# Conformer convolution and its layer norm: a tenth tap moved off VectorE, the mean's channel sums and the squares' sums moved to TensorE

## The chip, the cores and the metric

The kernel runs on one core of one Trainium2 chip. The metric is the device time of one execution in microseconds (us). A core has TensorE (PE, with its weight loads shown apart as PEld), VectorE (DVE), ScalarE (ACT), GpSimd (POOL) and the DMA queues, most of them fed by SyncE (SP). An engine works through its own instructions in order, and semaphores tie the engines together.

## What is computed

A model of two conformer and attention layers, followed by a mixer layer, on 512 latent tokens and 256 context tokens with 1024 channels. The part that matters is the first layer's convolution module:

```
u = h @ w_pw1 + b_pw1
a, g = split(u, 2)
v = a * sigmoid(g)
v = dwconv(v, w_dw, b_dw)            # 31 taps along the tokens, one weight for each tap and channel
v = silu(layernorm(v, ln_g, ln_b))   # mean and variance over the 1024 channels of a token
y = v @ w_pw2 + b_pw2
```

Latent and context tokens go through it as two separate sequences of 512 and 256.

## The kernel before

**Layout.** Activations lie with the channels on the 128 partitions: a tile of the 8 channel tiles is 128 channels by 768 tokens (512 latent, 256 context). Sums over channels are therefore sums over partitions, which TensorE makes by a matmul with a matrix of ones (`ones`), and sums over the 8 tiles.

**Stage `pw1`.** `pw1_pe` multiplies the 16 weight chunks of `w_pw1` (two for each channel tile: gate, then value) in three fp32r products each (high and low parts, lines 593 to 595). Between the chunks it works off the modulation weights (`ada`, line 818), two or three groups of 64 matmul records in each period. `sigmoid` on ScalarE and `gated` on VectorE (line 1267) make the gated tile `vp[j]`. Then the 31 taps of tile j are divided as follows: one on TensorE with a diagonal matrix (`taps_pe`, line 880), which opens the sum in PSUM; 9 (`POOL_TAPS`) as a product on ScalarE (`tap_act`, line 1311, two instructions for each tap) with the sum on GpSimd (`sum_pool`, line 1322, 8 sums for each tile); and 21 (`DVE_TAPS`) on VectorE (line 1290, two instructions for each tap, of 512 and of 256 tokens). VectorE puts `gated(j + 1)` after its 12th tap and ends the tile by adding GpSimd's sum (line 1294). `copy_conv` on ScalarE (line 1371) then writes `cv[j]` and frees the PSUM pair for the value chunk of tile j + 2. Products wait in a ring of three buffers (`PT_RING`), so a tap product waits for the sum three before it. ScalarE's order in a tile is five taps, the sigmoid, a weight chunk's high part, `copy_conv(j - 1)`, the modulation rows with their DMAs, the other taps, and the second weight chunk before the last of them. GpSimd also makes the low parts of the weights (line 535), the diagonal for TensorE (line 1394), and, one tile late, the running sum of `cv` over the channel tiles (`cv_sum_pool`).

**Between `pw1` and `pw2`.** After a last pair of transposes that wait for modulation values read back by DMA (line 842), `mean_pe` multiplies `ones` with `cv_sum` (tiles 0 to 6) and, once `cv[7]` is there, with `cv[7]` (line 1385). `mean_dve` subtracts the mean from the 8 tiles (line 1434), `square_act` squares them (line 1008), `add_square_dve` adds the squares tile by tile (line 1017), and `norm_pe` sums them over the channels with `ones` (line 988), so that all 128 partitions hold the same 768 sums. ScalarE takes the root of all 128 x 768 (line 1158), VectorE the reciprocal of all of it (line 1186), and VectorE multiplies tile by tile (line 1197). ScalarE applies gain, shift and SiLU (line 1176) and writes the high part (line 1178), VectorE the low part (line 1193), and `pw2`'s matmuls start with the first tile.

**The rest.** After `pw2` comes a long row of matmul stages; their weights are streamed chunk by chunk: SP loads `raw`, ScalarE makes the high part, GpSimd the low part, TensorE multiplies.

Of the kernel before, what the change touches and what calls it, by code (L numbers as in the profile page):

```python
# [6 lines left out]
P = 128  # L7
D = 1024
# [8 lines left out]
TAPS = 31  # L17
PAD = TAPS // 2
PE_TAPS = 1
POOL_TAPS = 9  # L20
PT_RING = 3
EPS = 1e-6
GN_EPS = 64e-5
# [129 lines left out]
class Program:  # L153

    def __init__(self, nc, ctx, A):
# [9 lines left out]
        def at(name, offset, shape, dt=F32):  # L166
            return nc.alloc_sbuf_tensor_at(name, [P] + shape, dt, offset=offset)
# [18 lines left out]
        self.cv_sum = at("cv_sum", r_wlo, [2, HALF * P])[:, :, KD * P:HALF * P]  # L186
# [193 lines left out]
def build_in(nc, ctx, A, out, stop):  # L380
# [770 lines left out]

    def norm_act(act, name):
        i, pair, w = NN[name], norm_pair(name), NORM_W[name]
        if name not in EARLY.values():
            for k in range(KD):
                square_act(act, name, k)
        act.wait_ge(stat_ready, done(i + 1))
        act.activation(M.n_y[:, 0, 0:w], M.pair(pair, 0, w), ACT.Sqrt, scale=1.0 / D, bias=eps_col)\
            .then_inc(rms_ready, 1)
        if name == "n10":  # L1160
            for g in (0, 1):
                group_act(act, g, 0, g * 1024)
            high_first(act)
            act.wait_ge(mod_ready, done(1))
        for k in range(KD):
            act.wait_ge(t_ready, done(8 * i + k + 1))

            if k >= 2:
                act.wait_ge(x_ready, done(8 * i + k - 1))
            else:  # L1170
                act.wait_ge(rstd_ready, done(i + 1))
            fn = ACT.Silu if name == "ln" else ACT.Identity
            dst = M.n_y[:, k % 2, :]
            for s, t0, t1 in norm_segs(name):
                scale, shift = scale_of(name, k, s)
                ins = act.activation(dst[:, t0:t1], M.n_t[:, k % 2, t0:t1], fn, scale=scale, bias=shift)
            act.drain()
            act.activation(M.x_hi[:, k, 0:w], M.n_y[:, k % 2, 0:w], ACT.Copy).then_inc(y_ready, 1)

    def norm_dve(dve, name):  # L1180
        i, pair, w = NN[name], norm_pair(name), NORM_W[name]
        if name not in EARLY.values():
            for k in range(KD):
                add_square_dve(dve, name, k)
        dve.wait_ge(rms_ready, done(i + 1))
        dve.reciprocal(M.pair(pair, 0, w), M.n_y[:, 0, 0:w]).then_inc(rstd_ready, 1)  # L1186
        dve.wait_ge(rstd_ready, done(i + 1))
# [12 lines left out]
        low(KD - 1)  # L1200
# [196 lines left out]
    def cv_sum_pool(pool, j):  # L1397
        def halves(k):
            return M.cv[:, k, :].rearrange("p (a b) -> p a b", a=2)

        if j < 1:
            return
        pool.wait_ge(cv_ready, done(j + 1))
        if j == 1:
            pool.tensor_tensor(M.cv_sum, halves(0), halves(1), ALU.add).then_inc(cv_sum, 1)
            return
        pool.wait_ge(cv_sum, done(j - 1))
        pool.tensor_tensor(M.cv_sum, M.cv_sum, halves(j), ALU.add).then_inc(cv_sum, 1)

    def pw1_pool(pool):  # L1410
        pool.wait_ge(start_c, done(3 + KD))
# [2 lines left out]
        for j in range(8):  # L1414
            for n in range(1, 5):
                sum_pool(pool, j, n)
            if j < 6:
                low_stream(pool, "pw1", 2 * j + 4, 2 * j + 5)
            sum_pool(pool, j, 5)
            sum_pool(pool, j, 6)  # L1420
            cv_sum_pool(pool, j - 1)
            if j < 7:
                diag_pool(pool, j + 1)
            for n in range(7, POOL_TAPS):
                sum_pool(pool, j, n)
            if j < 6:
                low_stream(pool, "pw1", 2 * j + 5, 2 * j + 6)
# [1593 lines left out]

    @block.tensor
    def _(pe):
        prime(pe, [pe_taps, mod_t, tile_done, ada_used, start_t, stat_ready, mu_ready, mem_t, out_t, mix_stat, ffn2_stat, rope_r, turn_t, att_s, att_t, att_o, T_S.sem])
        start_pe(pe)
        for st in order:
            if st == "ln":
                mean_pe(pe)
            if st == "n10":
                ada_pe(pe)  # L3030
            elif st in NN:
                norm_pe(pe, st)
            if st == "w_in":
                w_in_pe(pe)
# [101 lines left out]
```

## Time and profile before

| | |
|---|---|
| median of 3 runs | 2482.0 us (2481.49 to 2483.29) |
| profiled execution, its own time | 2475.95 us |
| its span (first to last instruction) | 2474.2 us |
| TensorE busy | 2249.4 us, 91% of the span |
| VectorE, ScalarE, GpSimd busy | 1201.3, 985.8, 814.3 us |
| mean granted TensorE clock | 0.954 of full speed |

The rows of the trace give times from the start of the span. A timeline row is: start, length, engine, line, operation, output <- inputs, shapes, count of merged instructions, and in brackets the idle time of the engine ahead of it with what ended it.
### The profile page before, as it was taken

The numbers are of one execution on the slowest core, as the hardware profiler recorded it, in microseconds if no ns is written. First come the engines' busy times: TensorE is split into PE (matmuls) and PEld (weight loads), VectorE is DVE, ScalarE is ACT, GpSimd is POOL, SyncE is SP. The second block draws the span as 40 slices with busy tenths as digits, with TensorE's granted clock in tenths as the row PEclk, the third lists the DMA queues.
The fourth block names the chain that finished last, engine by engine and source line by source line (L and its number), as shares of the span: only waits on it lengthen the run. The fifth ranks groups of instructions, "written<-read, shape, count | busy, mean of one in ns | idle before, by whom it ended". The sixth has DMA issues, their size and how long they took to land.

```text
span 2474.2 us, 36592 instructions
## 1 busy us (share of the span) xinstructions
PE 2249.4 (91%) x14159; PEld 1844.7 (75%) x14159; DVE 1201.3 (49%) x2038; ACT 985.8 (40%) x1634; POOL 814.3 (33%) x391
## 2 busy tenths in 40 slices
PE   5999297999999996989979999989988879999998
PEld 4887186888888885867758888877756767778777
DVE  4799834432034325468554313458565435541441
ACT  5555445332133314368544324444453213441441
POOL 1788221323223221300124434433302113444443
PEclk9999598999999998999989999999988879999999
DMA  8887011222122221200023333332200002233332
GB/s 267 268 261 240 19 52 43 60 68 71 58 60 60 73 63 48 77 18 1 27 85 94 104 87 99 108 103 77 81 1 2 2 1 77 85 106 88 87 101 86
DMA packets 337086, 204.54 MB, mean 83 GB/s; under 512 B 5869, under 2 KB 335159, under 8 KB 336951
## 3 DMA queue, kind: packets, MB, share of 16 engines
q1 hardware_dynamic: 331915, 194.02, 26.2%
q10 hardware_dynamic: 5036, 8.66, 1.1%
q8 instruction: 91, 1.49, 0.3%
q14 instruction: 44, 0.36, 0.0%
HBM read 200.47 MB, written 2.19 MB: 82 GB/s over the span
## 4 chain that ended last, share of the span: by engine, by line
PE 49%; issue 27%; DVE 11%; POOL 8%; ACT 2%; DVEq 1%; SPq 1%; DMA 1%; ACTq 0%; POOLq 0%
PE ps L593 14%; PE ps L594 14%; PE ps L595 14%; POOL w_lo L535 7%; DVE ps L1290 6%; PE ps L1622 1%; DVE ps L1186 1%; DVE m L2820 1%; PE ps L1650 1%; PE ps L2639 1%; DMA ada_x<-in_ada_w 1%; SPq L696 0%; PE ps L2635 0%; PE ps L2626 0%; PE ps L818 0%
## 5 line engine op out<-in xcount | busy, mean ns | idle before, releaser
L535 POOL TENSOR_TENSOR w_lo<-raw,w_hi 128x1024 fp32r<-128x1024 f32 (+1 forms) x253 | 646.5, 2556 | 1394.4 <-ACT w_hi L565 1378.4
L593 PE MATMUL ps<-x_hi,w_hi 128*128 128x512 f32 (+1 forms) x1864 | 679.4, 364 | 63.3 <-DVE x_lo L1193 50.6
L594 PE MATMUL ps<-x_lo,w_hi 128*128 128x512 f32 (+1 forms) x1864 | 666.8, 358 | 0.0
L595 PE MATMUL ps<-x_hi,w_lo 128*128 128x512 f32 (+1 forms) x1864 | 665.8, 357 | 0.0
L565 ACT ACTIVATE w_hi<-raw 128x1024 fp32r<-128x1024 f32 (+1 forms) x251 | 280.6, 1118 | 559.4 <-PE ps L595 553.9
L593 PEld LDWEIGHTS ps<-x_hi,w_hi 128*128 128x128 f32 x1864 | 355.7, 191 | 134.2 <-issue 60.6
L594 PEld LDWEIGHTS ps<-x_lo,w_hi 128*128 128x128 f32 x1864 | 356.0, 191 | 52.9 <-issue 3.8
L595 PEld LDWEIGHTS ps<-x_hi,w_lo 128*128 128x128 f32 x1864 | 355.4, 191 | 51.2
L1523 DVE SCALAR_TENSOR_TENSOR f_a<-ps,prm,f_a 128x511 f32<-128x511 f32 (+2 forms) x176 | 116.2, 681 | 356.3 <-ACT f_b L1488 345.4
L593 PE MATMUL ps<-g_hi,w_hi 128*128 128x512 f32 (+1 forms) x704 | 256.9, 365 | 2.1 <-POOL w_lo L535 1.4
L594 PE MATMUL ps<-g_lo,w_hi 128*128 128x512 f32 (+1 forms) x704 | 255.8, 363 | 0.0
L595 PE MATMUL ps<-g_hi,w_lo 128*128 128x512 f32 (+1 forms) x704 | 255.4, 363 | 0.0
L1290 DVE SCALAR_TENSOR_TENSOR ps<-vp,prm,ps 128x512 f32<-128x512 f32 x336 | 177.8, 616 | 2.5 <-PE ps L880 2.5
L1488 ACT ACTIVATE f_a<-ps,prm 128x512 f32<-128x512 f32 (+1 forms) x66 | 56.2, 851 | 300.2 <-PE ps L595 212.2
L593 PEld LDWEIGHTS ps<-g_hi,w_hi 128*128 128x128 f32 x704 | 132.8, 189 | 25.4 <-POOL w_lo L535 3.0
L595 PEld LDWEIGHTS ps<-g_hi,w_lo 128*128 128x128 f32 x704 | 132.7, 188 | 21.2
L593 PE MATMUL ps<-xg_hi,w_hi 128*128 128x512 f32 x352 | 139.7, 397 | 9.3 <-POOL w_lo L535 9.3
L594 PEld LDWEIGHTS ps<-g_lo,w_hi 128*128 128x128 f32 x704 | 132.9, 189 | 20.1
L595 PE MATMUL ps<-xg_hi,w_lo 128*128 128x512 f32 x352 | 137.2, 390 | 0.0
L594 PE MATMUL ps<-xg_lo,w_hi 128*128 128x512 f32 x352 | 137.2, 390 | 0.0
L1322 POOL TENSOR_TENSOR pc<-pc,pt 128x768 f32<-128x768 f32 x64 | 118.0, 1843 | 27.2 <-ACT pt L1311 21.9
L1555 DVE SCALAR_TENSOR_TENSOR h<-ps,mods,h 128x512 f32<-128x512 f32 (+1 forms) x48 | 30.3, 659 | 188.3 <-PE ps L595 188.3
(363 smaller groups left out, 2907.5 us busy)
## 6 DMA issues: line engine op xcount, KB each, us to landing
raw<-in_ffn_w_up SPq DMA_DIRECT2D x88, 512.0 KB, 3.8
ada_tail<-in_ada_w SPq DMA_DIRECT2D x22, 1024.0 KB, 7.4
raw<-in_ffn_w_down SPq DMA_DIRECT2D x32, 704.0 KB, 4.4
raw<-in_w_up SPq DMA_DIRECT2D x44, 512.0 KB, 3.8
ada_s<-in_ada_w SPq DMA_DIRECT2D x20, 1024.0 KB, 7.8
raw<-in_conv_w_pw SPq DMA_DIRECT2D x24, 512.0 KB, 6.4
raw<-in_w_down SPq DMA_DIRECT2D x16, 704.0 KB, 4.4
raw<-in_w_in SPq DMA_DIRECT2D x17, 512.0 KB, 3.9
```

The lines of the kernel that those rows point to most:

```text
L535: pool.tensor_tensor(M.w_lo[:, slot, 0:K * P], M.raw[:, slot, 0:K * P], M.w_hi[:, slot, 0:K * P].bitcast(F32), ALU.subtract).then_inc(lo_r ...
L565: act.activation(M.w_hi[:, slot, 0:K * P], M.raw[:, slot, 0:K * P], ACT.Copy).then_inc(hi_ready, 1)
L593: pe.matmul(o, wh, hi[:, k, t0:t0 + tn], start=(k == 0), stop=False)
L594: pe.matmul(o, wh, lo[:, k, t0:t0 + tn], start=False, stop=False)
L595: return pe.matmul(o, wl, hi[:, k, t0:t0 + tn], start=False, stop=(k == K - 1))
L1186: dve.reciprocal(M.pair(pair, 0, w), M.n_y[:, 0, 0:w]).then_inc(rstd_ready, 1)
L1290: dve.scalar_tensor_tensor(out=o, in0=src, scalar=w, in1=o, op0=ALU.mult, op1=ALU.add)\
L1322: pool.tensor_tensor(acc, acc, M.pt[:, m % PT_RING, :], ALU.add).then_inc(pool_tap, 1)
L1488: ins = act.activation(dst[:, slot, 0:w], M.pair(pr, 0, w), ACT.Identity, scale=ffn_cols(b, zero_tap, t, hf, j), bias=ffn_cols(b, None, t, ...
L1523: ins = dve.scalar_tensor_tensor(out=dst[:, slot, o0:o1], in0=M.pair(pr, o0 + sh, o1 + sh), scalar=ffn_cols(b, tap, t, hf, j), in1=dst[:, ...
L1555: dve.scalar_tensor_tensor(out=o, in0=src, scalar=M.mods[:, 48 * b + 40 + m, s:s + 1], in1=o, op0=ALU.mult, op1=ALU.add)
L1622: mm = pe.matmul(M.pair(u % 2, off, off + n), lhs, rhs, start=first, stop=True, skip_group_check=True)
```

## The change

Three edits, all in the convolution module.

1. `POOL_TAPS` is 10 instead of 9, so VectorE has 20 taps for each tile, ScalarE 10 products and GpSimd 9 sums. ScalarE's second weight chunk stays ahead of the last product.
2. The running sum `cv_sum` on GpSimd goes away (7 sums, their semaphore and their buffer). `mean_pe` multiplies `ones` with each of `cv[0]` to `cv[7]`.
3. In the layer norm the squares are no longer added by VectorE. TensorE multiplies each tile of squares, as the moving operand in six blocks of 128 tokens, with a stationary matrix of 128 x 6 that has ones in one column and zeros elsewhere (`pick6`), and so puts the sums of block b into row b of a PSUM tile of 6 x 128. Root and reciprocal work on 6 x 128. Six matmuls with a row of the identity, stretched to 6 x 128, put each row back on all 128 partitions.

```
-POOL_TAPS = 9
+POOL_TAPS = 10
...
-        pe.wait_ge(cv_sum, done(6))
-        for t0, t1, half in ((0, 384, 0), (384, SEQ, 1), (SEQ, TOK, 1)):
-            pe.matmul(M.pair(pair, t0, t1), ones, M.cv_sum[:, half, ...], start=t0 != 384, ...)
-        pe.wait_ge(cv_ready, done(KD))
-        for t0, tn in BOTH:
-            mm = pe.matmul(M.pair(pair, t0, t0 + tn), ones, M.cv[:, KD - 1, t0:t0 + tn], ...)
+        for k in range(KD):
+            pe.wait_ge(cv_ready, done(k + 1))
+            for t0, tn in BOTH:
+                mm = pe.matmul(M.pair(pair, t0, t0 + tn), ones, M.cv[:, k, t0:t0 + tn], start=(k == 0),
+                               stop=(k == KD - 1))
         mm.then_inc(mu_ready, 1)
+
+    def ln_pe(pe):
+        i = NN["ln"]
+        pe.wait_ge(evac, done(NORM_Q["ln"]))
+        for k in range(KD):
+            pe.wait_ge(sq_ready, done(8 * i + k + 1))
+            for b in range(6):
+                mm = pe.matmul(ln_rows(), M.pick6[:, 5 - b:11 - b], M.n_sq[:, k % 2, b * P:(b + 1) * P],
+                               start=(k == 0 and b == 0), stop=(k == KD - 1 and b == 5))
+            mm.then_inc(sq_used if k < KD - 1 else stat_ready, 1)
+        pe.wait_ge(ln_rt, done(1))
+        for b in range(6):
+            mm = pe.matmul(M.pair(norm_pair("ln"), b * P, (b + 1) * P), ident[0:6, b:b + 1].to_broadcast([6, P]),
+                           ln_row(0), start=True, stop=True)
+        mm.then_inc(ln_back, 1)
+
+    def ln_square_act(act, k):
+        ...
+        act.wait_ge(cv_cent, done(k + 1))
+        if k >= 2:
+            act.wait_ge(sq_used, done(7 * i + k - 1))
+        act.activation(M.n_sq[:, k % 2, :], M.cv[:, k, :], ACT.Square).then_inc(sq_ready, 1)
+
+    def ln_root_act(act):
+        act.wait_ge(stat_ready, done(NN["ln"] + 1))
+        act.activation(ln_row(1), ln_rows(), ACT.Sqrt, scale=1.0 / D, bias=M.one[0:6, 0:1]).then_inc(ln_sd, 1)
+
+    def ln_root_dve(dve):
+        dve.wait_ge(ln_sd, done(1))
+        dve.reciprocal(ln_row(0), ln_row(1)).then_inc(ln_rt, 1)
+        dve.wait_ge(ln_back, done(1))
...
             if k >= 2:
                 act.wait_ge(x_ready, done(8 * i + k - 1))
-            else:
-                act.wait_ge(rstd_ready, done(i + 1))
+            elif name != "ln":
+                act.wait_ge(rstd_ready, done(i + (i < 2)))
...
-            sum_pool(pool, j, 5)
-            sum_pool(pool, j, 6)
-            cv_sum_pool(pool, j - 1)
+            for n in range(5, 8):
+                sum_pool(pool, j, n)
             if j < 7:
                 diag_pool(pool, j + 1)
-            for n in range(7, POOL_TAPS):
+            for n in range(8, POOL_TAPS):
                 sum_pool(pool, j, n)
...
+        pool.memset(M.pick6[:, :], 0.0)
+        pool.drain()
+        pool.memset(M.pick6[:, 5:6], 1.0)
         pool.drain().then_inc(zero_ready, 1)
```

The last four lines stand at the very start of GpSimd's program; SP and ScalarE wait for `zero_ready`. For `ln`, `ln_square_act` and `ln_root_act` take the place of the squares and the root in `norm_act`, and `ln_root_dve` that of the additions and the reciprocal in `norm_dve`.

## Rows read from the trace of the kernel before

**Rows 1.** Chain of work that ended last, from 106.5 to 306 us, by line

```profile
by line: DVE ps L1290 74.5%; issue 6.3%; DVE cv L1434 3.5%; DVE n_t L1017 3.4%; DVE vp L1267 3.1%; DVE ps L1186 2.5%; PE ps L1385 1.5%; PE ps L988 1.5%; ACT L1176 0.6%; DVE ps L1294 0.6%; ACTq L1177 0.5%; DVE x_lo L1193 0.5%; ACT cv L1371 0
```

**Rows 2.** Timeline of VectorE in `pw1`: starts of tiles 1, 2 and 7

```profile
106.51 12.70 DVE L1290 SCALAR_TENSOR_TENSOR ps<-vp,prm,ps 128x512 f32<-128x512 f32 x24 [0.23 <-PE ps L880]
...
130.61 12.70 DVE L1290 SCALAR_TENSOR_TENSOR ps<-vp,prm,ps 128x512 f32<-128x512 f32 x24
...
251.11 22.14 DVE L1290 SCALAR_TENSOR_TENSOR ps<-vp,prm,ps 128x512 f32<-128x512 f32 x42
```

**Rows 3.** Timeline of TensorE in `pw1`: taps of tiles 1, 3 and 7, and a wait

```profile
104.94 1.46 PE L880 MATMUL ps<-vp,diag 128*128 128x512 f32 x4
...
151.05 1.46 PE L880 MATMUL ps<-vp,diag 128*128 128x512 f32 x4
...
155.97 0.47 PE L593 MATMUL ps<-x_hi,w_hi 128*128 128x512 f32 x1 [1.58 <-ACTq L1373]
...
240.80 2.48 PE L880 MATMUL ps<-vp,diag 128*128 128x512 f32 x4 [2.06 <-DVE vp L1267]
```

**Rows 4.** Groups by line and form, 70 to 275 us: busy, mean ns, idle before

```profile
L1322 POOL TENSOR_TENSOR pc<-pc,pt 128x768 f32<-128x768 f32 x64 | 118.0, 1843 | 27.2 <-ACT pt L1311 21.9
L535 POOL TENSOR_TENSOR w_lo<-raw,w_hi 128x1024 fp32r<-128x1024 f32 x16 | 38.3, 2398 | 25.7 <-ACT w_hi L565 25.7
...
L1311 ACT ACTIVATE pt<-vp,prm 128x512 f32<-128x512 f32 x64 | 45.7, 714 | 16.8 <-issue 9.4 <-POOL pc L1322 7.4
```

**Rows 5.** Timeline of all engines, 256 to 306 us

```profile
256.84 3.77 POOL L1322 TENSOR_TENSOR pc<-pc,pt 128x768 f32<-128x768 f32 x2 [6.16 <-ACT pt L1311]
259.02 0.33 ACTq L871 DMA_DIRECT2D mod_t<-mod_scratch  x1
...
261.32 0.50 PE L842 MATMUL ps<-kb,mod_t 80*128 80x80 f32 x2 [15.46 <-DMA mod_t<-mod_scratch]
...
275.23 2.93 PE L1385 MATMUL ps<-cv,kb 128*128 128x512 f32 x4 [9.81 <-ACT cv L1371]
...
278.19 7.01 DVE L1434 SCALAR_TENSOR_TENSOR cv<-ps,cv 128x768 f32<-128x768 f32 x8 [2.79 <-PE ps L1385]
279.24 0.84 ACT L1008 ACTIVATE n_t<-cv 128x768 f32<-128x768 f32 x1 [4.06 <-DVE cv L1434]
...
291.27 1.28 ACT L1158 ACT_TABLE_LOAD   x1
...
292.59 2.90 PE L988 MATMUL ps<-n_t,kb 128*128 128x512 f32 x4 [14.43 <-DVE n_t L1017]
...
296.46 4.96 DVE L1186 RECIPROCAL ps<-n_y 128x768 f32<-128x768 f32 x1 [4.02 <-ACT n_y L1158]
...
301.50 1.28 ACT L1176 ACT_TABLE_LOAD   x1 [5.07 <-DVE ps L1186]
...
305.87 0.76 PE L593 MATMUL ps<-x_hi,w_hi 128*128 128x512 f32 x1 [10.38 <-DVE x_lo L1193]
```

**Rows 6.** Busy time in stretches: PE, PEld, DVE, ACT, POOL, granted clock, DMA, GB/s

```profile
305.87:309.40 3.53, 3.53 (x10) 2.95 (x11) 3.35 (x4) 3.40 (x4) 0.00 (x0) 0.50 0.00 0
309.40:320.00 10.60, 10.08 (x59) 8.69 (x58) 8.43 (x10) 8.26 (x10) 0.00 (x0) 0.99 0.00 0
...
2025.00:2030.00 5.00, 5.00 (x25) 4.57 (x24) 0.00 (x0) 0.00 (x0) 0.00 (x0) 0.50 0.00 0
```

**Rows 7.** Timeline of TensorE elsewhere: fp32 records over 128 columns, weights of 6 columns

```profile
1084.74 0.60 PE L1637 MATMUL ps<-kb,p 128*128 128x128 f32 x4
...
1734.02 0.09 PEld L2152 LDWEIGHTS ps<-hot,relb 33*6 33x6 f32 x2 [0.35 <-issue]
```

**Rows 8.** Groups by line and form, whole span: a smaller reciprocal and a smaller copy

```profile
L1127 DVE RECIPROCAL rm<-rm 128x256 f32<-128x256 f32 x1 | 1.8, 1754 | 2.9 <-ACT rm L1118 2.9
L856 ACT ACTIVATE mod_rows<-ps 128x256 f32<-128x256 f32 x12 | 4.6, 383 | 6.7 <-PE ps L818 3.2 <-issue 2.6 <-ACT cv L1371 0.9
```

**Rows 9.** Chain of work that ended last, the first microseconds of the kernel

```profile
1.64 0.23 POOLq L2959
```

More of the change, by code:

```diff
@@ L426, in build_in @@
     pe_taps = sem("pe_taps")
-    cv_sum = sem("cv_sum")
+    ln_sd = sem("ln_sd")
+    ln_rt = sem("ln_rt")
+    ln_back = sem("ln_back")
     mu_ready = sem("mu_ready")
@@ L1153, in norm_act @@
         i, pair, w = NN[name], norm_pair(name), NORM_W[name]
-        if name not in EARLY.values():
+        if name == "ln":
             for k in range(KD):
[L1156 to L1159, printed above, removed]
+                ln_square_act(act, k)
+            ln_root_act(act)
+        else:
+            if name not in EARLY.values():
+                for k in range(KD):
+                    square_act(act, name, k)
+            act.wait_ge(stat_ready, done(i + 1))
+            act.activation(M.n_y[:, 0, 0:w], M.pair(pair, 0, w), ACT.Sqrt, scale=1.0 / D, bias=eps_col)\
+                .then_inc(rms_ready, 1)
         if name == "n10":
@@ L1181, in norm_dve @@
         i, pair, w = NN[name], norm_pair(name), NORM_W[name]
[L1182 to L1187, printed above, removed]
+        if name == "ln":
+            ln_root_dve(dve)
+        else:
+            if name not in EARLY.values():
+                for k in range(KD):
+                    add_square_dve(dve, name, k)
+            dve.wait_ge(rms_ready, done(i + (i < 2)))
+            dve.reciprocal(M.pair(pair, 0, w), M.n_y[:, 0, 0:w]).then_inc(rstd_ready, 1)
+            dve.wait_ge(rstd_ready, done(i + (i < 2)))
         if name == "n10":
@@ L1378, in mean_pe @@
         pe.wait_ge(evac, done(Q0["pw2"] - 4))
-        pe.wait_ge(cv_sum, done(6))
-        for t0, t1, half in ((0, 384, 0), (384, SEQ, 1), (SEQ, TOK, 1)):
-            pe.matmul(M.pair(pair, t0, t1), ones, M.cv_sum[:, half, t0 - 384 * half:t1 - 384 * half], start=t0 != 384,
-                      stop=False, skip_group_check=True)
-        pe.wait_ge(cv_ready, done(KD))
-        for t0, tn in BOTH:
-            mm = pe.matmul(M.pair(pair, t0, t0 + tn), ones, M.cv[:, KD - 1, t0:t0 + tn], start=False, stop=True,
-                           skip_group_check=True)
@@ L1387, in mean_pe, with ln_rows, ln_row @@
-        mm.then_inc(mu_ready, 1)
+        for k in range(KD):
+            pe.wait_ge(cv_ready, done(k + 1))
+            for t0, tn in BOTH:
+                mm = pe.matmul(M.pair(pair, t0, t0 + tn), ones, M.cv[:, k, t0:t0 + tn], start=(k == 0),
+                               stop=(k == KD - 1))
+        mm.then_inc(mu_ready, 1)
+    def ln_rows():
+        return M.pair((Q0["pw2"] + 1) % 4, 0, P)[0:6, :]
+    def ln_row(which):
+        return M.gate[0:6, 1, which * P:(which + 1) * P]
+    def ln_pe(pe):
+        i = NN["ln"]
+        pe.wait_ge(evac, done(NORM_Q["ln"]))
+        for k in range(KD):
+            pe.wait_ge(sq_ready, done(8 * i + k + 1))
[8 more added lines that the diff above has]
+        mm.then_inc(ln_back, 1)
@@ new lines, in ln_square_act @@
+    def ln_square_act(act, k):
+        i = NN["ln"]
+        if k == 0:
+            act.wait_ge(x_ready, done(8 * i))
+        act.wait_ge(cv_cent, done(k + 1))
[5 more added lines that the diff above has]
+        act.activation(ln_row(1), ln_rows(), ACT.Sqrt, scale=1.0 / D, bias=M.one[0:6, 0:1]).then_inc(ln_sd, 1)
@@ L1395, in diag_pool @@
         ins.then_inc(diag_ready, 1)
[L1397 to L1408, printed above, removed]
     def pw1_pool(pool):
@@ L2951, in _ @@
     def _(pool):
-        prime(pool, [P_S.sem, lo_ready, zero_ready, diag_ready, cv_sum, pool_tap, tap_prod])
+        prime(pool, [P_S.sem, lo_ready, zero_ready, diag_ready, pool_tap, tap_prod])
         pool.memset(M.p_rows[:, PT - 1, :], 0.0)
@@ L3028, in _ @@
                 mean_pe(pe)
+                ln_pe(pe)
             if st == "n10":
                 ada_pe(pe)
-            elif st in NN:
+            elif st in NN and st != "ln":
                 norm_pe(pe, st)
@@ L3069, in _ @@
     def _(dve):
-        prime(dve, [sq_used, evac, mod_ready, rstd_ready, t_ready, x_ready, h_ready, v_ready, tap_done, cv_cent,
+        prime(dve, [ln_rt, sq_used, evac, mod_ready, rstd_ready, t_ready, x_ready, h_ready, v_ready, tap_done, cv_cent,
                     taps_ready, prod_ready, g_ready, out_c, MIX.x, MIX.sum, MEMO.x, MEMO.sum, FFN2.x, FFN2.sum,
```

6 lines of the change are left out of this document (3 added, 3 removed).

## The prediction

> **What bounds the kernel now.** I read the page first (TensorE busy for 91% of the span), then the chain of waits over the part that the change touches, then the timelines. The chain [rows 1] shows that this part, unlike the rest, is not TensorE's: 74.5% of the 200 us from 106.5 to 306 us are VectorE's taps, and most of what is left is the layer norm, in which one engine at a time works. The timeline of VectorE [rows 2] shows the taps back to back: tile 1 starts at 106.51, tile 2 at 130.61, so a tile takes 24.10 us, and a tap (two instructions) takes 22.14 / 21 = 1.05 us. Tile 1 had to wait 0.23 us for TensorE's tap: up to there TensorE sets the pace. The timeline of TensorE [rows 3] shows it close behind afterwards: from its taps of tile 1 (104.94) to those of tile 3 (151.05) there are 46.11 us for two tiles, without a wait of note, 23.05 for each. From then on it waits for `copy_conv`, 1.58 us at 155.97. After the last tap there is a serial path [rows 5]: the mean ends at 278.16 (275.23 + 2.93), the squares' sums at 295.49, the reciprocal at 301.42, and `pw2` starts at 305.87. From there on TensorE is busy again (10.08 of 10.60 us, [rows 6]), so whatever `pw2`'s start gains, the end of the kernel gains: its weights are ready long before, and nothing in the later stages changes.
>
> **The tap.** It comes off each of 8 tiles on VectorE. For tile 0 it gives nothing: VectorE ends it earlier and then waits for TensorE's tap at 104.94 plus 1.46 [rows 3], so tile 1 still starts at 106.5. For tiles 1 to 7 it gives 1.05 each, 7.35 in all, if the others keep a period of 24.10 - 1.05 = 23.05. TensorE needs 23.05, exactly as much. Its waits for `copy_conv` go away when VectorE is earlier, since that is what they wait for, so it can hold this pace; I take off 0.15 for tiles at which the two meet: 7.2. ScalarE has one more tap, 0.71 for the 512 half plus an estimated 0.5 for the other [rows 4], of a tile in which it is busy for little more than half the time. GpSimd gets a sum of 1.84 and loses the running sum, an addition over the same 128 x 768, so it stays even: 9 x 1.84 + 2 x 2.40 [rows 4] plus a small diagonal, some 22 us of 23.05. The second weight chunk's high part slips by one product; it waits for a TensorE chunk anyway. Bounds of this term: 0 (rival C) and 8.05, the 7.35 plus the 0.23 and what tile 0 might still give.
>
> **The mean.** `cv_sum` was hidden, so taking it from GpSimd gains nothing by itself. What was exposed is one product over 768 tokens at 1.2 GHz, 2.93 us [rows 5]. Now there are eight. `cv[0]` to `cv[6]` can start when the transposes at line 842 are through, and those wait for a DMA that ScalarE issues behind its last products. That DMA went out at 259.02, when GpSimd's sums that started at 256.84 had begun to free the ring, and TensorE had its data 2.30 us later [rows 5]. In the changed kernel tile 7's sums start 6 x 1.05 = 6.3 earlier, at 250.5, and the tenth product waits for two of them (3.7), so the DMA goes out at about 254.3, the transposes run at 256.6 and the products start at 257.2. At 1.2 GHz a product costs 2.56 (2.93 without the last pass's tail, which I put at 0.35); at 2.4 GHz 1.39 (from 1.46 for the same four records, [rows 3]). The clock rises after some work: `pw2`'s first matmuls ran 3.53 us at 0.50 and then at 0.99 [rows 6]. With 3.5 us slow (1.4 products) and 5.6 products fast (7.8), TensorE is through `cv[6]` at 268.5. `cv[7]` is there at 275.2 - 7.2 = 268.0, so its product follows at once and ends at 270.1. Before, the mean came 2.96 us after `cv[7]` was there, now 2.1: gain 0.85. If the products stayed at 1.2 GHz throughout they would end at 257.2 + 8 x 2.56 + 0.35 = 278.0, and all that the taps gave would be gone. Bounds: +1.5 (7 products done in time, the last one fast) and -7.1.
>
> **The squares' sums.** From the first subtraction (278.19) to the end of the sum over channels (295.49) took 17.30. Seven additions on VectorE, about 1.06 apart, go. Now the first square is made as before, 1.05 behind the subtraction, and takes 0.84 [rows 5]; then 8 tiles of 6 matmuls, 96 records of 128 columns. Four such records with other weights took 0.60 [rows 7], so 0.11 apart behind a tail of 0.27; loading 6 columns takes 0.09 for two and hides. I take 0.115: 1.38 for a tile, 11.0 for all, plus 0.2. ScalarE's 0.84 for a square is hidden behind it, since two buffers alternate and TensorE is the slower. TensorE pauses for 1.9 us before it begins. After a pause of 2.06 us its four tap records took 2.48, not 1.46 [rows 3], so such a pause can drop the clock for a while; that costs 1.0 to 1.8, and I put in 0.9. Together 1.9 + 11.2 + 0.9 = 14.0: gain 3.3. Bounds: gain 4.2 (no dip), and at 1.2 GHz throughout 20.5 + 0.35 in place of 11.2 + 0.9, loss 5.4.
>
> **A rule on this clock.** A stretch elsewhere kept TensorE busy for 5.00 of 5.00 us and its granted clock stayed at 0.50 [rows 6], and those were 25 records of small tiles. So a busy engine is no warrant of the full clock; that is rival B. The Trainium skill, "TensorE: Matmul & The Clock Gate", section on the HAM clock gate, says that the gate follows how busy TensorE has been and that sustained work releases it. By that rule the squares' sums run at 2.4 GHz, as in my forecast; by the row they could run at 1.2 GHz, and the sum would be rival B's.
>
> **Root, reciprocal, back.** Before, 295.49 to 301.46: 5.97. Now the root over 128 columns: between nothing and the 0.90 of 768, nearest 0.38 for 256 [rows 8]; I take 0.40 with its bias operand. The reciprocal: 4.96 for 768 [rows 5] and 1.75 for 256 [rows 8] give 0.95 for 128. Six matmuls back: 12 records x 0.115 + 0.2 = 1.58 (3.0 at 1.2 GHz). With four handovers of 0.05: 3.1, gain 2.85. Then ScalarE's table load for SiLU (1.28, [rows 5]) ran only after the reciprocal, because its wait for `rstd_ready` stood ahead of it; the load for the root at 291.27 had no such second wait and ran ahead of its data. The change takes the second wait away, so the load hides behind reciprocal and matmuls: SiLU starts 0.88 after the product begins, not 1.32, gain 0.44. The multiplications, SiLU, high and low parts are unchanged.
>
> **The start.** Two memsets and a drain are added ahead of `zero_ready`, and the drain there is on the chain at 0.23 [rows 9]. SP's parameter loads wait for it: loss 0.25. Bounds 0 and 0.5.
>
> **Sum.** 7.2 + 0.85 + 3.3 + 2.85 + 0.44 - 0.25 = 14.4 us. Against the profiled execution that is 2475.95 - 14.4 = 2461.5; that execution lies 6 us below the median of the runs, and on the median it gives 2482.0 - 14.4 = 2467.6.
>
> **Rivals.** About 5 us (0.2%) is what a measurement can tell from no change.
>
> A, the forecast: 2467.6, with a range of its own of 2464.5 to 2470.
>
> B, the clock stays at 1.2 GHz during the squares' sums and the matmuls back, because short records with 6 columns of weights do not keep it up. It costs 8.7 and 1.4: gain 4.3, time 2477.7. For it speaks the busy stretch at 0.50; against it that weights of 6 columns load quickly, so that TensorE streams nearly without a break, and that TensorE comes to them at full clock.
>
> C, the conv stage does not follow VectorE: GpSimd with its 22 us and idle gaps (27.2 us before its sums in 8 tiles, 3.4 in each, [rows 4]) or TensorE's 23.05 holds the period at 24.1. The 7.2 go, time 2474.8. Against it: those idle gaps wait for ScalarE's products, which wait for VectorE's end of the tile before, so they shrink with it.
>
> D, the mean's products stay at 1.2 GHz: they end at 278.0, the gain is 14.4 - 7.9 = 6.5, time 2475.5. Against it: 11 us of unbroken full-width matmuls.
>
> E, on the other side: each of the 96 records waits for its weights and for the one before it, so that a record costs its whole length at 1.2 GHz, which I bound by twice the 0.27 tail, 0.5 with the load. Then the squares' sums take 96 x 0.5 = 48, 36 more: time 2504, slower. It decides above 0.115 + (14.4 + 5) / 96 = 0.32 us for a record. Against it: the four records at 0.11 apart.
>
> **How the numbers follow.** A 0.62, B 0.12, C 0.10, D 0.08, E 0.03; 0.05 for something that I don't see, half of it slower. Faster by over 0.2% means under 2477.0: A, C, D, and a third of B, 0.84. Within 0.2%: two thirds of B and some of the rest, 0.11. Slower: 0.05. The range reaches from the lower bounds of the terms (the squares without the dip, a fast mean) to C and D: 2463.5 to 2476.0, which leaves out B, E and a little at the low end.
>
> **What would show it.** Line 1290 in 320 instructions, VectorE's tiles 23.05 apart from 106.5 on, tile 7's last sum at about 267; TensorE's waits for `copy_conv` gone. Eight products of `mean_pe` from 257 on, at full clock from about 261, the last one ending 2.1 us after `cv[7]`. 96 records of the squares' sums 0.115 apart in about 11 us; a reciprocal of 6x128 at 0.95; a table load directly behind the root; first matmul of `pw2` at 305.87 - 14.4 = 291.5. The prediction is wrong if the granted clock reads 0.50 between 272 and 284 us, if GpSimd has no idle time between 110 and 250 us, or if later stages lose what `pw2`'s start has won.

## The result, and the profile after

| | before | after | ratio, 95% interval |
|---|---|---|---|
| on the first chip, median | 2481.87 us (2481.49 to 2483.29) | 2466.3 us (2464.96 to 2467.01) | 0.9938 [0.9924, 0.9952] |
| on another chip, median | 2482.14 us (2475.54 to 2484.15) | 2464.88 us (2463.63 to 2467.17) | 0.9937 [0.9923, 0.9950] |
| profiled execution, its own time | 2475.95 us | 2467.01 us | |
| its span | 2474.2 us | 2465.2 us | |

The kernel is 15.6 us faster in the runs (0.6%); 14.4 were forecast. The two profiled spans are only 9.0 us apart: the profiled execution before was among the shortest of its kernel, 6 us under the median, and the one after was not. The stage itself shows the whole gain, and the difference lies in two places outside it. Timeline of VectorE after: the first gated tile, then the starts of tiles 1, 2, 3 and 7 and the last sum.

```profile
72.92 1.14 DVE L1277 SCALAR_TENSOR_TENSOR vp<-ps,prm,gate 128x512 f32<-128x512 f32 x2 [5.66 <-PE ps L597]
...
108.95 12.70 DVE L1300 SCALAR_TENSOR_TENSOR ps<-vp,prm,ps 128x512 f32<-128x512 f32 x24 [1.28 <-PE ps L882]
...
132.00 12.69 DVE L1300 SCALAR_TENSOR_TENSOR ps<-vp,prm,ps 128x512 f32<-128x512 f32 x24
...
155.05 12.70 DVE L1300 SCALAR_TENSOR_TENSOR ps<-vp,prm,ps 128x512 f32<-128x512 f32 x24
...
247.26 21.09 DVE L1300 SCALAR_TENSOR_TENSOR ps<-vp,prm,ps 128x512 f32<-128x512 f32 x40
268.38 0.96 DVE L1304 TENSOR_TENSOR ps<-pc,ps 128x768 f32<-128x768 f32 x1
```

**Everything starts 2.44 us later.** Tile 1 starts at 108.95 instead of 106.51 [rows 2], and the first gated tile at 72.92. In the profile before that one stood at 70.48, so the shift is older than any tap. Only 0.16 of it are the change's (SP's first parameter load is issued at 2.04, before at 1.88, behind the added memsets). Most of the rest comes from the clock; this is TensorE's row for a block of modulation weights, before and then after:

```profile
34.40 1.96 PE L818 MATMUL ps<-ada_x,sc 128*32 128x128 f32 x64 [3.18 <-DMA ada_x<-in_ada_w]
```

```profile
34.61 3.30 PE L820 MATMUL ps<-ada_x,sc 128*32 128x128 f32 x64 [4.70 <-DMA ada_x<-in_ada_w]
```

A longer pause ahead, and the same 64 records take 3.30 instead of 1.96 us. With them the first norm's reciprocal starts 1.84 us later (40.65, before 38.81), the 0.16 included. The other 0.6 is VectorE's, in the two small instructions for that norm's gain (line 922 before, 924 after), which last from start to end 2.11 us instead of 1.48; why is open. None of this is work of the edits: the kernel with the tap alone, which has no added memsets, also began at 72.60, and one with the whole change and an eleventh tap at 70.58. The slow block alone does not decide it: the kernel with the records doubled had it too (3.27 us) and began at 71.01, because the two small instructions took 0.27 us there. Some 4.3 us more go far behind the stage, most of them in stretches of lower clock; one of them is here, the same 62 records in both (windows of all engines, before and then after; the third number from the end is the granted clock, 1.00 and 0.83). It costs 2.8 us:

```profile
1673.20:1690.61 17.41, 14.61 (x62) 11.12 (x61) 12.66 (x10) 7.43 (x14) 7.65 (x4) 1.00 0.32 90
```

```profile
1659.95:1680.15 20.20, 17.41 (x62) 13.16 (x61) 12.62 (x10) 7.42 (x14) 7.60 (x4) 0.83 0.28 78
```

So I measure the stage by itself: from the first gated tile (start of the first instruction of `gated`) to ScalarE's first SiLU. That took 302.80 - 70.48 = 232.32 before and 289.45 - 72.92 = 216.53 after: 15.8 less, and with the 0.16 at the start 15.6, which is what the runs show. On the other chip it took 216.33. (The 6.6 by which the two spans show less than 15.6 are the 2.3 of the start and these 4.3.)

**The conv tiles** are 23.05 apart (132.00 to 155.05), as forecast. GpSimd, in a tile without a gap, from a group of four sums to the same one of the next tile, takes 22.66:

```profile
173.60 7.78 POOL L1332 TENSOR_TENSOR pc<-pc,pt 128x768 f32<-128x768 f32 x4
...
196.26 7.79 POOL L1332 TENSOR_TENSOR pc<-pc,pt 128x768 f32<-128x768 f32 x4
```

**The mean and the layer norm**, timeline of all engines after:

```profile
259.63 0.50 PE L844 MATMUL ps<-kb,mod_t 80*128 80x80 f32 x2 [18.18 <-DMA mod_t<-mod_scratch]
259.92 12.42 PE L1392 MATMUL ps<-cv,kb 128*128 128x512 f32 x32
...
272.37 7.01 DVE L1468 SCALAR_TENSOR_TENSOR cv<-ps,cv 128x768 f32<-128x768 f32 x8 [1.63 <-PE ps L1392]
...
274.43 10.64 PE L1410 MATMUL ps<-n_sq,pick 128*6 128x128 f32 x96 [2.10 <-ACT n_sq L1426]
...
285.11 0.36 ACT L1430 ACTIVATE gate<-ps,one 6x128 f32<-6x128 f32 x1 [0.42 <-PE ps L1410]
285.48 1.28 ACT L1183 ACT_TABLE_LOAD   x1
285.50 0.94 DVE L1434 RECIPROCAL gate<-gate 6x128 f32<-6x128 f32 x1 [6.12 <-ACT gate L1430]
...
286.50 1.93 PE L1415 MATMUL ps<-gate,kb 6*128 6x128 f32 x12 [1.42 <-DVE gate L1434]
288.46 1.82 DVE L1207 TENSOR_TENSOR n_t<-ps,cv 128x768 f32<-128x768 f32 x2 [2.02 <-PE ps L1415]
289.45 1.03 ACT L1183 ACTIVATE n_y<-n_t,prm 128x768 f32<-128x768 f32 x1 [2.69 <-DVE n_t L1207]
...
292.54 0.76 PE L595 MATMUL ps<-x_hi,w_hi 128*128 128x512 f32 x1 [4.11 <-DVE x_lo L1203]
```

The mean ends at 272.34, 2.06 after ScalarE has ended `cv[7]` (270.28). The 96 records stand without a gap, 10.64 us; the table load for SiLU runs beside the reciprocal; `pw2` starts at 292.54. Windows over the mean's products, the squares' records, the matmuls back and `pw2`'s first ones:

```profile
259.92:264.00 4.08, 4.08 (x9) 2.10 (x7) 4.08 (x9) 0.00 (x0) 3.94 (x3) 0.53 0.01 2
264.00:272.34 8.34, 8.33 (x27) 4.75 (x25) 6.47 (x21) 0.90 (x1) 3.25 (x2) 1.00 0.42 127
274.43:285.07 10.64, 10.64 (x96) 8.36 (x96) 4.95 (x6) 6.97 (x8) 0.00 (x0) 1.00 0.01 2
286.50:288.43 1.93, 1.93 (x12) 1.63 (x12) 0.00 (x0) 0.27 (x1) 0.00 (x0) 0.79 0.00 0
292.54:297.79 5.25, 5.25 (x15) 4.38 (x16) 5.06 (x6) 4.99 (x6) 0.00 (x0) 0.50 0.00 0
```

The clock came up 3.8 us into the mean's products and was at its full level for all of the squares' records, across the pause of 2.10 us between the two. `pw2`'s first matmuls ran at 0.50 for 5.25 us, longer than before (3.53, [rows 6]), but that cost nothing. From the first SiLU to the reciprocal of the next norm it takes 82.1 us in both kernels (302.80 to 384.89 before, 289.45 to 371.55 after):

```profile
384.89 4.96 DVE L1186 RECIPROCAL ps<-n_y 128x768 f32<-128x768 f32 x1 [4.01 <-ACT n_y L1158]
```

```profile
371.55 4.96 DVE L1196 RECIPROCAL ps<-n_y 128x768 f32<-128x768 f32 x1 [4.02 <-ACT n_y L1165]
```

### The profile page after: what moved, and what is told of

Read it like the earlier page. It is cut to its first block, busy times and chain, and to the rows that moved or that the text cites. A ratio compares the mean times of both kernels' runs of the same rounds, so it can differ in the third digit from the quotient of the medians.

```text
span 2465.2 us, 36840 instructions
## 1 busy us (share of the span) xinstructions
PE 2269.7 (92%) x14285; PEld 1862.9 (76%) x14285; DVE 1182.5 (48%) x2015; ACT 992.9 (40%) x1650; POOL 817.6 (33%) x395
## 4 chain that ended last, share of the span: by engine, by line
PE 51%; issue 27%; DVE 10%; POOL 8%; ACT 2%; DVEq 1%; SPq 1%; DMA 1%; ACTq 0%; POOLq 0%
PE ps L595 14%; PE ps L596 14%; PE ps L597 14%; POOL w_lo L537 7%; DVE ps L1300 5%; PE ps L1656 1%; PE ps L2673 1%; DVE m L2854 1%; PE ps L1684 1%; PE ps L2660 1%; DMA ada_x<-in_ada_w 1%; PE ps L1392 0%; SPq L698 0%; PE ps L820 0%; PE ps L2669 0%
## 5 line engine op out<-in xcount | busy, mean ns | idle before, releaser
L1300 DVE SCALAR_TENSOR_TENSOR ps<-vp,prm,ps 128x512 f32<-128x512 f32 x320 | 169.3, 613 | 3.5 <-PE ps L882 3.5
L1332 POOL TENSOR_TENSOR pc<-pc,pt 128x768 f32<-128x768 f32 x72 | 132.6, 1842 | 17.5 <-ACT pt L1321 10.4
```

Source lines behind the costliest of these rows:

```text
L1300: dve.scalar_tensor_tensor(out=o, in0=src, scalar=w, in1=o, op0=ALU.mult, op1=ALU.add)\
L1332: pool.tensor_tensor(acc, acc, M.pt[:, m % PT_RING, :], ALU.add).then_inc(pool_tap, 1)
```

## The experiments

All were timed in 5 rounds beside the kernel before. "Stage" is the length from the first gated tile to SiLU, from the profile of each, one execution. The changed kernel's two profiles agree in it within 0.2 us; the medians of the runs differ from what the stages say by up to 3.8 us, either way (mean only: 3.8 us slower in the runs, with an interval that begins at 1.0000, and no change in the stage). Those parts lie outside the stage and are not explained here.

| kernel | median (before beside it) | ratio, 95% interval | stage | against before |
|---|---|---|---|---|
| before | | | 232.32 | |
| tap only | 2473.82 (2479.99) | 0.9977 [0.9968, 0.9986] | 229.18 | -3.1 |
| mean only | 2483.83 (2479.99) | 1.0009 [1.0000, 1.0018] | 232.31 | 0.0 |
| layer norm only | 2472.93 (2479.99) | 0.9974 [0.9962, 0.9986] | 227.55 | -4.8 |
| mean and layer norm (no tap) | 2470.20 (2479.99) | 0.9964 [0.9952, 0.9976] | 223.09 | -9.2 |
| all three | 2464.88 (2482.14) | 0.9937 [0.9923, 0.9950] | 216.33 | -16.0 |
| additions back on VectorE | 2471.10 (2479.88) | 0.9957 [0.9944, 0.9971] | 222.40 | -9.9 |
| records doubled | 2476.54 (2479.88) | 0.9983 [0.9974, 0.9992] | 228.78 | -3.5 |
| eleven taps | 2471.82 (2479.88) | 0.9966 [0.9954, 0.9978] | 224.43 | -7.9 |
| fp32r squares | 2463.81 (2479.88) | 0.9933 [0.9919, 0.9946] | 213.69 | -18.6 |
| fp32r squares and back | 2464.57 (2482.14) | 0.9936 [0.9922, 0.9951] | 212.29 | -20.0 |

**Tap only** (`cv_sum` stays on GpSimd, which now has 9 sums and the running sum).

```
-POOL_TAPS = 9
+POOL_TAPS = 10
```

> The tenth tap alone: the running sum stays on GpSimd, mean and layer norm as before. GpSimd then has 9 sums, the running sum, two low parts and the diagonal in a tile, 9 x 1.84 + 1.85 + 4.8 + 0.6 = 23.85 us against VectorE's 23.05. Theory 1: GpSimd's sums are done some 6 us ahead of the tile's end, so a lag of 0.8 a tile is absorbed over 7 tiles and all 7.3 us are gained: about 2474.6, tiles 23.05 apart. Theory 2: the stage goes at GpSimd's pace, tiles 23.85 apart, gain 1.8: about 2480.1.

Its VectorE:

```profile
199.95 0.96 DVE L1294 TENSOR_TENSOR ps<-pc,ps 128x768 f32<-128x768 f32 x1
...
216.26 1.15 DVE L1267 SCALAR_TENSOR_TENSOR vp<-ps,prm,gate 128x512 f32<-128x512 f32 x2 [1.50 <-PE ps L595]
225.84 0.96 DVE L1294 TENSOR_TENSOR ps<-pc,ps 128x768 f32<-128x768 f32 x1
```

Its GpSimd, the same group of four sums in two tiles:

```profile
175.91 7.76 POOL L1322 TENSOR_TENSOR pc<-pc,pt 128x768 f32<-128x768 f32 x4
...
200.32 7.72 POOL L1322 TENSOR_TENSOR pc<-pc,pt 128x768 f32<-128x768 f32 x4
```

The stage gains 3.1, not 7.3. GpSimd has no idle time between these two rows, and a tile takes it 24.41 us, more than the pace of 23.05. VectorE's tiles still end 23.05 apart up to 199.95: GpSimd started with a lead, and four tiles use it up. The next tile ends 25.89 later, behind waits of 1.15 for TensorE's tap and of 1.50 for its value chunk. ScalarE and TensorE show how GpSimd comes to hold them up:

```profile
202.17 1.12 ACT L1311 ACTIVATE pt<-vp,prm 128x512 f32<-128x512 f32 x2 [3.00 <-POOL pc L1322]
204.93 0.89 ACT L1371 ACTIVATE cv<-ps,prm 128x768 f32<-128x768 f32 x1
206.04 0.69 PE L593 MATMUL ps<-x_hi,w_hi 128*128 128x512 f32 x1 [2.21 <-ACTq L1373]
```

ScalarE's fifth product of the tile waits 3.00 us for a buffer of the ring, that is, for a sum of GpSimd's. The sigmoid, the weight chunk's high part and `copy_conv` stand behind it in ScalarE's order, so `copy_conv` runs at 204.93, though VectorE had ended the tile at 200.91. TensorE's value chunk waits 2.21 us for it, and its first matmuls run at a granted clock of 0.50 (0.63 us each). The chunk's low part was no cause: GpSimd had ended it at 200.37. What follows: the edit to the mean, which takes one sum of 1.84 off each tile, is what pays for most of the tap.

**Mean only.**

```
-        pe.wait_ge(cv_sum, done(6))
...
+        for k in range(KD):
+            pe.wait_ge(cv_ready, done(k + 1))
```

> The eight products of the mean alone: 9 products on ScalarE and GpSimd, layer norm as before. Theory 1: tiles 0 to 6 are through before cv[7] comes, and the last product runs at full clock: gain 0.9 to 1.4, about 2480.8. Theory 2 (the clock stays at 1.2 GHz): products end near 261.8 + 20.8 = 282.6 instead of 278.2, loss 4.4, about 2486.3.

TensorE's products of the mean:

```profile
263.77 10.74 PE L1381 MATMUL ps<-cv,kb 128*128 128x512 f32 x28
277.43 2.93 PE L1381 MATMUL ps<-cv,kb 128*128 128x512 f32 x4 [2.92 <-ACT cv L1370]
```

No gain in the stage. Seven products brought the clock up (0.86 over their 10.74 us), TensorE then waited 2.92 us for `cv[7]`, and its product took 2.93 again, granted clock 0.50, as before [rows 5]. Both theories missed this: theory 1 had the last product at full clock, theory 2 had the clock low throughout.

**Layer norm only**, the third edit alone.

> The layer norm in rows alone: 9 products, running sum on GpSimd and short mean as before. Theory 1: the layer norm's own terms add up as in the changed kernel, 4.6 + 2.6 + 0.3 - 0.2 = 7.3 gained: 2474.6, squares' sums 1.31 a tile. Theory 2: the mean's eight products also warm TensorE for them; after a mean of only 2.93 us and a pause the squares' sums begin at 1.2 GHz and lose 1 to 3 us: 2475.6 to 2477.6, granted clock 0.50 in their first part.

```profile
275.31 2.93 PE L1397 MATMUL ps<-cv,kb 128*128 128x512 f32 x4 [9.79 <-ACT cv L1383]
280.33 13.32 PE L1415 MATMUL ps<-n_sq,pick 128*6 128x128 f32 x96 [2.10 <-ACT n_sq L1431]
```

The same 96 records take 13.32 us, of which the first 5.5 ran at a granted clock of 0.50, against 10.64 behind eight products. The clock was at 0.50 for the single product ahead of the pause already, so it did not fall in the pause: it had not come up. The twelve records back took 2.02. So the layer norm's edit is worth 4.8 by itself and 7.9 behind the new mean (stages: from the first subtraction to SiLU 24.61 before, 19.86 here, 16.76 in the kernel without the tap).

**Mean and layer norm, no tap.**

```
-POOL_TAPS = 10
+POOL_TAPS = 9
```

> The changed kernel with 9 products instead of 10: mean and layer norm changed, VectorE with 21 taps. Theory 1: the parts are independent, 15.6 - 7.3 = 8.3 gained: 2473.6. Theory 2: the tap and the removed running sum only work together (GpSimd), then this kernel gains the same 8.3 but the tap alone less than 7.3, and e1 shows it.

```profile
264.24 11.94 PE L1392 MATMUL ps<-cv,kb 128*128 128x512 f32 x28
277.53 1.56 PE L1392 MATMUL ps<-cv,kb 128*128 128x512 f32 x4 [1.35 <-ACT cv L1381]
281.18 10.64 PE L1410 MATMUL ps<-n_sq,pick 128*6 128x128 f32 x96 [2.10 <-ACT n_sq L1426]
293.25 1.60 PE L1415 MATMUL ps<-gate,kb 6*128 6x128 f32 x12 [1.42 <-DVE gate L1434]
```

The pause ahead of `cv[7]`'s product is 1.35 us here, the product takes 1.56 at full clock, and everything behind it runs at full clock too. The two edits give 9.2; the tap adds 6.6 to them. That is the 7.3 of its tiles less 0.45, by which the mean ends later behind the last sum (3.99 us to the first subtraction, 3.54 here), and 0.33 in the matmuls back (1.93 and 1.60).

**Additions back on VectorE** (the squares added as before, then one set of six matmuls with `pick6`; root, reciprocal and back as in the changed kernel).

```
-        for k in range(KD):
-            pe.wait_ge(sq_ready, done(8 * i + k + 1))
-            for b in range(6):
-                mm = pe.matmul(ln_rows(), M.pick6[:, 5 - b:11 - b], M.n_sq[:, k % 2, b * P:(b + 1) * P],
...
+        pe.wait_ge(sq_used, done(7 * i + 7))
+        for b in range(6):
+            mm = pe.matmul(ln_rows(), M.pick6[:, 5 - b:11 - b], M.n_t[:, 0, b * P:(b + 1) * P],
...
```

> The changed kernel with the squares added on VectorE as before (7 additions, 1.06 apart) and one set of 6 matmuls on their sum; root, reciprocal and return in rows stay. Theory 1: the end of the squares' sums comes 14.4 us after the first subtraction, plus 1.3 for the matmuls at 2.4 GHz or 2.6 at 1.2 GHz, so 15.7 to 17 instead of 12.7; and the return costs 1.9 or 3.2: 3 to 5.6 us slower than the changed kernel, about 2469.3 to 2471.9. Theory 2: the additions were no bound and only the root in rows gains: same as the changed kernel, 2466.3.

```profile
288.36 2.72 PE L1411 MATMUL ps<-n_t,pick 128*6 128x128 f32 x12 [14.44 <-DVE n_t L1019]
292.50 2.92 PE L1416 MATMUL ps<-gate,kb 6*128 6x128 f32 x12 [1.42 <-DVE gate L1435]
```

The sums end at 291.08, 17.1 after the first subtraction (273.96), against 12.70. TensorE stood for 14.44 us, and so both sets of twelve records ran at 1.2 GHz (2.72 and 2.92, granted clock 0.50). The stage is 5.9 longer than the changed kernel's first profile: 4.4 from the sums, 1.0 from the matmuls back, 0.5 from the mean (4.46 us behind the last sum, not 3.99).

**Records doubled**: each matmul of the squares' sums is made twice, and the root halves the sum.

```
-            for b in range(6):
+            for b, r in [(b, r) for b in range(6) for r in (0, 1)]:
```

> The changed kernel with each of the 48 matmuls of the squares' sums made twice (192 records, the root's scale halved, the result the same). Theory 1: TensorE's record pace of 0.109 sets this part: 10.5 us more, 2476.8. Theory 2: ScalarE's squares or VectorE's subtractions set it and half the records are hidden: 3 to 6 us more.

```profile
272.95 22.79 PE L1410 MATMUL ps<-n_sq,pick 128*6 128x128 f32 x192 [2.10 <-ACT n_sq L1426]
```

```profile
273.60:276.00 2.40, 2.40 (x14) 1.46 (x12) 2.40 (x3) 0.00 (x0) 0.00 (x0) 0.50 0.00 0
```

22.79 - 10.64 = 12.15 for 96 more records, and the stage grows by 12.3. Of the 12.15, 10.5 are the 96 records at 0.109, as theory 1 had it; the other 1.7 is a dip of the clock. It fell to 0.50 at 273.1, right behind the pause of 2.10, and came back at 276.5 (before the window shown and after it, 14 records in 2.40 us). This is the pause behind eight products that had no dip in the changed kernel. The records set this part: with half of them hidden behind ScalarE's squares or VectorE's subtractions the cost would have been less than 10.5.

**Eleven taps.**

```
-POOL_TAPS = 10
+POOL_TAPS = 11
```

> The changed kernel with an eleventh product (VectorE 19 taps, GpSimd 10 sums). VectorE needs 22.0 us a tile, TensorE 23.05, GpSimd 10 x 1.84 + 4.8 + 0.6 = 23.85. Theory 1: the stage goes at TensorE's pace, GpSimd's lag is absorbed: same as the changed kernel, tiles 23.05 apart, with waits of VectorE for TensorE's taps; 1 us gained on tile 7, 2465.3. Theory 2: GpSimd sets the pace, 23.85 apart, 4 to 6 us slower than the changed kernel, 2470 to 2472.

VectorE's tile 3, and TensorE's mean:

```profile
155.09 12.70 DVE L1300 SCALAR_TENSOR_TENSOR ps<-vp,prm,ps 128x512 f32<-128x512 f32 x24 [2.33 <-PE ps L882]
```

```profile
265.17 0.50 PE L844 MATMUL ps<-kb,mod_t 80*128 80x80 f32 x2 [18.08 <-DMA mod_t<-mod_scratch]
265.47 12.29 PE L1392 MATMUL ps<-cv,kb 128*128 128x512 f32 x32
```

GpSimd, the same group again:

```profile
153.54 7.72 POOL L1332 TENSOR_TENSOR pc<-pc,pt 128x768 f32<-128x768 f32 x4
...
178.22 7.78 POOL L1332 TENSOR_TENSOR pc<-pc,pt 128x768 f32<-128x768 f32 x4
```

It takes 24.68 for a tile without a gap, and VectorE, with 22.0 of work, waits: 1.4 to 2.3 us for TensorE's tap at six tiles and 2.1 for its value chunks. Tiles 1 to 7 start 24.08 apart on average (106.58 to 251.04), as before the change. And the DMA that the transposes need goes out behind the last products, at 262.85, so the mean ends 4.7 after `cv[7]` is there, not 2.1. On this division of the work the tenth tap is the last that fits.

**fp32r squares**: the squares are rounded to fp32r, and `pick6` is a copy in fp32r, so a matmul is one record (48 instead of 96).

```
-                mm = pe.matmul(ln_rows(), M.pick6[:, 5 - b:11 - b], M.n_sq[:, k % 2, b * P:(b + 1) * P],
+                mm = pe.matmul(ln_rows(), M.pick6r[:, 5 - b:11 - b], M.n_sq_r[:, k % 2, b * P:(b + 1) * P],
```

> The changed kernel with the squares and the 128 x 6 matrix in fp32r, which makes one record of each matmul instead of two (48 records); the squares are rounded to fp32r. Theory 1: TensorE's records set the part; with 48 of them VectorE's subtractions, 0.88 a tile, set it: it ends about 1.9 + 7 x 0.88 + 0.5 = 8.6 after the first subtraction instead of 12.7, 4.1 us gained, 2462.2. Theory 2: a record over 128 columns of fp32r costs as much as two of fp32 for want of columns: no gain.

```profile
275.99 0.52 PE L1412 MATMUL ps<-n_sq_r,pick6r 128*6 128x128 f32 x6 [0.34 <-ACT n_sq_r L1428]
...
283.10 2.92 PE L1417 MATMUL ps<-gate,kb 6*128 6x128 f32 x12 [1.84 <-DVE gate L1436]
```

The root starts 9.3 after the first subtraction, not 12.7: ScalarE's 0.87 for a square now sets the pace, and TensorE pauses 0.34 between six records. After three such bursts the clock fell (granted clock 0.50 from 276.85 on, 4.41 us to the end), and the matmuls back took 2.92 instead of 1.93. That the short pauses made it fall is argued, not shown: in the kernel with the records doubled it fell without any, though it came back after 3.4 us. Of 3.4 us the stage keeps 2.8. The conversion to fp32r added at the start puts SP's first parameter load at 2.55, not 2.04: 0.5 us that the stage leaves out, here and in the next version.

**fp32r squares and back**: in addition the row of 1/deviation and the identity's six columns are fp32r, so that the way back has six records.

```
-            mm = pe.matmul(M.pair(norm_pair("ln"), b * P, (b + 1) * P), ident[0:6, b:b + 1].to_broadcast([6, P]),
-                           ln_row(0), start=True, stop=True)
+            mm = pe.matmul(M.pair(norm_pair("ln"), b * P, (b + 1) * P), M.id6r[0:6, b:b + 1].to_broadcast([6, P]),
+                           M.gate_r[0:6, 1, 0:P], start=True, stop=True)
```

> The fp32r squares of the run before (48 records in place of 96, so ScalarE's 0.87 us a tile sets the pace) and the matmuls back in fp32r too: the row of 1/deviation is rounded to fp32r, and the six matmuls back are 6 records in place of 12; VectorE copies the identity's first 6 columns beforehand. In the fp32r-squares run the twelve records back took 2.92 us, against 1.93 in the changed kernel. Theory 1 (each record of 128 columns costs the same there, 0.24 us at the lower clock, whatever its type): 6 records take 1.5 us, SiLU starts 1.4 us earlier than in the fp32r-squares run, 3.8 us ahead of the changed kernel, and the time is 3 to 4 us under the changed kernel's on the same chip (ratio to the kernel before 0.992). Theory 2 (what the squares' part gains is given back, since TensorE's lighter work leaves a lower clock to pw2's first matmuls too): less than 1.5 us between the two, with pw2's first matmuls longer than in the changed kernel.

```profile
280.46 1.54 PE L1419 MATMUL ps<-gate_r,id6r 6*128 6x128 f32 x6 [1.84 <-DVE gate_r L1441]
```

The six records take 1.54 us, and the stage is 4.0 us shorter than the changed kernel's on the same chip, as theory 1 had it; `pw2`'s first matmuls are as slow in both (0.63 for the second one), so theory 2's reason is not there; with the 0.5 us at the start, 3.5 us should be left. But the runs don't show the gain: 2464.57 (2461.66 to 2468.55) against 2464.88 for **the changed kernel again**:

> The changed kernel as it is, beside the fp32r version on one chip. Both theories expect what its first runs gave: 15.6 us under the kernel before, a ratio of 0.9938 within 0.001 (some 2464 to 2467 us), and a squares' part of 12.7 us from the first subtraction to the end of the sums, with 1.9 us for the twelve matmuls back.

In the profiles the lead of 6.2 us (4.0 and an earlier start) is whole at the reciprocal of the next norm (365.21 against 371.45) and still 5.9 at one near 1740 us, and it is 2.4 at the one near 2090 us, so it goes in between, where the clock changes several times. Whether that is given back in each execution is open; the version is not shown to be faster.

## Why the prediction was right

Measured against the first gated tile of each profile, by the prediction's own terms:

| term | forecast | measured | from |
|---|---|---|---|
| tap | 7.2 | 7.34 | last sum at 273.28 before, 268.38 - 2.44 after |
| mean | 0.85 | 0.92 | 4.91 and 3.99 from the last sum's start to the first subtraction |
| squares' sums | 3.3 | 4.60 | 17.30 and 12.70 |
| root, reciprocal, back | 2.85 | 2.58 | 5.97 and 3.39 |
| table load for SiLU | 0.44 | 0.33 | 1.32 and 0.99 |
| start | -0.25 | -0.16 | SP's first parameter load |
| sum | 14.4 | 15.6 | runs: 15.6 |

**The tap**: right in all its steps. VectorE's period is 23.05, tile 0 gives nothing, TensorE's waits for `copy_conv` are gone, and GpSimd keeps idle time: 17.5 us ahead of its sums, less than the 27.2 of before [rows 4]. Rival C did not happen, but the two experiments with more on GpSimd show how near it is: at 22.66 us for a tile of GpSimd's the stage follows VectorE, at 24.41 it loses more than half of the gain, at 24.68 all of it. I had put GpSimd at some 22: nine sums of 1.84 start 1.93 apart where they are in a row, which makes the difference.

**The mean**: size and working are right. The products started at 259.92, less the 2.44 at 257.5 (257.2 forecast), the clock rose after 3.8 us (3.5), and they were through `cv[6]` 0.6 after `cv[7]` was there (0.5). What I had not seen is that the edit is worth nothing by itself: it makes the room on GpSimd that the tap needs, and its products bring up TensorE's clock for the squares. Alone, the three edits give 3.1, 0.0 and 4.8 in the stage (7.9); together they give 15.8. The medians of the runs are rougher and say the same: 6.2, -3.8 and 7.1 (9.4), and 15.6 to 17.3 together.

**The squares' sums** are the term that was mis-sized, by 1.3. I had put in 0.9 for a dip of the clock after a pause of 1.9, from the tap records behind a pause of 2.06 [rows 3]. The pause was 2.10 and there was no dip; a record took 0.109, not 0.115. That there was none is in part luck. Behind eight products and the same pause there was none in the changed kernel (both profiles), without the tap and with eleven taps, but one of 1.7 us with the records doubled, whose program is the same up to the pause (its eight products took 13.04 us, not 12.42, because the clock came up later in them). So the 0.9 was a fair price for a risk, and why the clock held in four profiles and fell in the fifth is not settled. With only one product ahead of the pause, run at 0.50, the cost was 2.7 us (layer norm only). The Trainium skill, "TensorE: Matmul & The Clock Gate", section on the HAM clock gate, has the clock follow how busy TensorE has been. These runs agree as far as the single product goes (13.32 us behind it, 10.64 behind eight); the dip with the records doubled is not told by that alone. Rival B, which the stretch of small tiles at 0.50 [rows 6] spoke for, did not occur: the records ran at 1.00 for 10.64 us, and with the records doubled for 19 us behind the dip.

**Root, reciprocal, back**: root 0.36 and reciprocal 0.94 as forecast; the twelve records back took 1.93, not 1.58, at a granted clock of 0.79; behind the same pause of 1.42 they took 1.60 in the kernel without the tap. Why it fell in one and not in the other is not settled.

**Later stages** did not eat the gain: the next norm's reciprocal is 15.8 us closer to the first gated tile (298.6 and 314.4 us). The 6.6 us by which the two profiles show less lie at the start and far behind, most of them in clock; the medians of the runs on two chips show 15.6 and 17.3.

## What to carry to other kernels

Ask of each edit what it frees for the others: here a sum that was hidden, and so worth nothing when taken away alone, was the room that the tap moved to GpSimd needed. Add up each engine's own work for a tile and hold it against the pace wanted, before work is moved to it: 22.66, 24.41 and 24.68 us against 23.05 made the difference between all, less than half and nothing; a surplus can hide for several tiles behind a lead before it shows, and it shows through what stands behind the waiting instruction in its engine's order (here `copy_conv` behind a tap's product). In a serial stretch, work on TensorE ahead of a short burst is worth more than its own time where it brings the clock up, and a faster form can lose part of its gain again when the clock falls in it, as both fp32r versions did.

## What the hardware showed that I had not expected

- Pauses ahead of full-width or short records: after 2.10 us (behind eight products, four profiles) and 1.35 us the work ran at full clock; after the same 2.10 us in a fifth profile (records doubled) the clock fell to 0.50 for 3.4 us; after 2.92 us (behind seven products) a product of four records took 2.93 instead of 1.56 us.
- The same row of products brought the clock up after 3.0 us (mean only), 3.8 (changed kernel) and 5.4 (no tap).
- Bursts of six records in 0.52 us with 0.34 between them ended at a granted clock of 0.50 in both fp32r versions, while 96 records without a gap held 1.00 over 10.64 us. Whether the gaps are the cause is open.
- ScalarE's root starts right behind its table load, in the last version:

```profile
277.78 1.28 ACT L1434 ACT_TABLE_LOAD   x1
279.08 0.36 ACT L1434 ACTIVATE gate<-ps,one 6x128 f32<-6x128 f32 x1
```

The Trainium skill, "ScalarE: Activation LUTs", section "What ACT_TABLE_LOAD costs", adds a drain of some 1380 ns to each load of some 1283 ns. The load agrees (1.28), the drain isn't there: the root starts 1.30 us after the load's start, so a switch of tables cost half of what the page has, and the measurement decides.
